# Gate and up as a two by two block product of seven products, in a decoder layer on one core

## The chip, the core and the metric

The kernel runs on one core of a Trainium2 chip. The time is the device time of one execution in microseconds. Three runs of the kernel before took 3130.09, 3134.56 and 3130.25 us; their median is 3130.25.

## What is computed

One layer of a decoder for 2048 tokens of width 1024, in float32:

```
h   = rmsnorm(x) @ w_in            -> q, k, v of two groups of heads
mix = [differential attention | stick-breaking attention]
x   = x + mix @ w_out
h2  = rmsnorm(x)
x   = x + (silu(h2 @ w_gate) * (h2 @ w_up)) @ w_down      # D_FF = 2816
out = rmsnorm(x)
```

The change touches the part from `mix @ w_out` on. Its matmuls take each float32 operand as a sum of two rounded ones, hi and lo (type float32r): a product is three matmuls, hi*hi, hi*lo and lo*hi, added up in PSUM.

## The kernel before

After projection and attention, the last part (`ffn_programs`, from L1402) goes over four blocks of 512 tokens. For each block:

- **project**: `mix` is transposed on TensorE, split into hi and lo, and multiplied with w_out in two halves of 512 output columns. The result is added to x.
- the sum is normalized, scaled into `natural`, transposed again (L1821 in block 0, L1830 in the others) and split by ScalarE (L1531) and VectorE (L1691) into `turned_hi` and `turned_lo`, 8 chunks of 128 rows x 512 tokens.
- **gate/up** (`gate_pair`, L1867): 22 tiles of 128 features. A tile is two products, gate and up, each of 8 chunks x 3 passes = 24 matmuls of 512 columns, into one PSUM bank. ScalarE takes Silu of the gate (L1543), VectorE multiplies with up (L1705), ScalarE rounds the result to `act_hi` (L1550) and VectorE makes `act_lo` (L1710). These two stay in SBUF for all 22 tiles.
- **down** (`passes`, L1788): twice 22 tiles of features, for each half of the output columns; per tile 4 token tiles x 3 passes = 12 matmuls of 512 columns. The first half of down is followed by the projection of the next block, then comes the second half, so that norms and transposes of the next block lie beside the second half.

The weights are one stream of items of 512 KB (`w_stream`), loaded by SP into two raw buffers in turn (L1444). ScalarE rounds an item to `w_hi` (128x1024, L1490, L1540, L1546) as soon as TensorE has done the item two before; VectorE subtracts to get `w_lo` (L1494, L1604); TensorE waits for `lo_split`. All engines run their instructions in the order in which they are written here, and semaphores count the steps: `multiplied` (TensorE's items), `hi_split`, `lo_split`, `silued`, `producted`. POOL has only the powers of the norms and the stores of the output in this part. `natural` of the next block is loaded early in gate/up (L1451) and x at the start of down.

Before this part begins, the last steps of attention are still under way: POOL multiplies the last weights (L1270), TensorE transposes them (L932), ScalarE copies them (L1024), TensorE multiplies with v (L946). `scalar_ahead` and `vector_ahead` split the first two items in that time (called at L1033 and L1192).

In the second part the block 0 opening is not covered by anything: TensorE has nothing else to do between its projection and its first gate matmul.

Of the kernel before, what the change touches and what calls it, by code (L numbers as in the profile page):

```python
# [22 lines left out]
P = 128  # L23
# [652 lines left out]
def attention_programs(nc, ctx, qk_scratch, v_scratch, lambdas_dram, g_mix_dram, g_mix, ident, ident_bf, causal, strict_drams,  # L676
# [3 lines left out]
    with memory:  # L680
# [516 lines left out]
        def gpsimd(pool, ahead):  # L1197
# [79 lines left out]
            def after(now):  # L1277
# [8 lines left out]
                for head in range(HEADS - 1):  # L1286
# [8 lines left out]
                    normed=S["normed"],  # L1295
                    g_ready=S["g_ready"])
# [6 lines left out]
HALF = D_MODEL // 2  # L1303
OUT_ITEMS = KC
GATE_ITEMS = 2 * FT
DOWN_ITEMS = FT // 2
PEELED = 3
PERIOD = OUT_ITEMS + GATE_ITEMS + 2 * DOWN_ITEMS
TOTAL = BLOCKS * PERIOD


def gate_item(b):
    return OUT_ITEMS + PERIOD * b


def out_item(b):
    return gate_item(b - 1) + GATE_ITEMS + DOWN_ITEMS if b else 0


def down_item(b, half):  # L1320

    between = OUT_ITEMS if b < BLOCKS - 1 else 0
    return gate_item(b) + GATE_ITEMS + half * (DOWN_ITEMS + between)


def stream_index(n):

    if n < OUT_ITEMS:
        return n
    b, at = divmod(n - OUT_ITEMS, PERIOD)  # L1330
    if at < GATE_ITEMS + DOWN_ITEMS:
        return OUT_ITEMS + at
    if b < BLOCKS - 1 and at < GATE_ITEMS + DOWN_ITEMS + OUT_ITEMS:
        return at - GATE_ITEMS - DOWN_ITEMS
    return at + (0 if b < BLOCKS - 1 else OUT_ITEMS)
# [6 lines left out]
def upper(b):  # L1342
    return 4 - lower(b)
# [10 lines left out]
def h2_bank(b, k):  # L1354
    return upper(b - 1) + k % 4 if b else k
# [6 lines left out]
def ahead_buffers(nc, ctx, H, low):  # L1362
# [5 lines left out]
    row = 4 * D_MODEL  # L1368
    small = low + (TPB + 3) * row
    F = dict(x_in=at("xin", [P, TPB, D_MODEL], keys), junk=[None, at("junk1", [P, HALF], queries)],  # L1370
             w_raw=[at(f"wraw{s}", [P, D_MODEL], values + s * row) for s in range(2)],
             natural=at("natural", [P, TPB, D_MODEL], low), g_final=at("gfinal", [P, D_MODEL], low + TPB * row),
             w_hi=[at("whi0", [P, D_MODEL], low + (TPB + 1) * row, F32R)],
             w_lo=[at("wlo0", [P, D_MODEL], low + (TPB + 2) * row, F32R)],
             g_ffn=at("gffn", [P, KC], small),
             w_loaded=[ctx.enter_context(nc.semaphore(f"f_w_loaded{s}")) for s in range(2)])
# [7 lines left out]
    assert small <= low + FENCE_BYTES  # L1384
# [17 lines left out]
def ffn_programs(nc, ctx, F, A, x, mix_scratch, w_stream, g_mix, limit, ident, out):  # L1402

    assert TOTAL % 2 == 0 and FT % 2 == 0
    memory = ExitStack()
    with memory:
        sb = lambda n, s, d=F32: memory.enter_context(nc.sbuf_tensor(n, s, d))
        sem = lambda n: ctx.enter_context(nc.semaphore(n))
        w_raw, natural, w_loaded = F["w_raw"], F["natural"], F["w_loaded"]
# [20 lines left out]

        done = lambda n: n + 2
        last = BLOCKS - 1


        turn_of = lambda which, b: b + which
        ready = KC - 1
# [588 lines left out]
```

## Time and profile before

| | |
|---|---|
| profiled execution | 3134.4 us, span 3132.6 us |
| TensorE busy | 3070.1 us, 98% |
| VectorE, ScalarE, POOL busy | 46%, 41%, 21% |
| gate/up stage of one block (four of them) | 239.36 us |
| down and projection between two gate/up stages | 170.30 us |
| mean granted TensorE clock | 0.996 of full speed |

The profile counts an engine as busy while an instruction of its own runs; TensorE's weight loads are counted apart, since they overlap its matmuls. The first 1472 us of the span are projection and attention, which stay as they are.

### The profile page before, as it was taken

The page shows a single profiled execution, that of the slowest core. Times are in us where ns is not written, and L with a number is a line of the kernel's source. Part 1 is how long each engine was busy: PE and PEld are TensorE (multiplying, and loading weights), DVE is VectorE, ACT ScalarE, POOL GpSimd, SP SyncE. Part 2 cuts the span into 40 slices and gives each one's busy share as a digit, 9 for nine tenths or more (in the row PEclk, how much of TensorE's full clock was granted, in tenths as well). Part 3 has the DMA queues.
Part 4 walks back from the last instruction along what each step waited for, and adds up shares of the span by engine and source line. Part 5 has one row for each costly group of instructions (what it writes and reads, how often), then busy time and mean ns, then how long its engine had stood idle before and what let it go on. Part 6 is the DMA issues. An engine that isn't in the chain of part 4 may idle for free.

```text
span 3132.6 us, 40561 instructions
## 1 busy us (share of the span) xinstructions
PE 3070.1 (98%) x16160; PEld 2584.0 (82%) x16160; DVE 1441.5 (46%) x1617; ACT 1294.6 (41%) x1968; POOL 669.4 (21%) x686
## 2 busy tenths in 40 slices
PE   7999999999999999999999999999999999999998
PEld 6887778787778999999888888888888888888887
DVE  6224420277676778777433333433334333343323
ACT  5122221367778887787322323322233222332222
POOL 1900000145446877775000000000000000000000
PEclk9999999999999999999999999999999999999999
DMA  5443353504444142220332322423224232233222
GB/s 197 126 122 102 94 138 92 134 18 95 108 108 93 30 108 57 53 85 15 121 99 95 121 94 94 148 96 125 94 94 148 94 119 101 96 107 108 94 101 94
DMA packets 136949, 314.77 MB, mean 100 GB/s; under 512 B 11745, under 2 KB 49377, under 8 KB 136673
## 3 DMA queue, kind: packets, MB, share of 16 engines
q1 hardware_dynamic: 134784, 305.84, 32.8%
q0 software_dynamic: 1728, 6.29, 0.5%
q8 instruction: 101, 1.65, 0.2%
q10 hardware_dynamic: 288, 0.59, 0.1%
q14 instruction: 48, 0.39, 0.0%
HBM read 253.96 MB, written 58.72 MB: 100 GB/s over the span
## 4 chain that ended last, share of the span: by engine, by line
PE 65%; DVE 7%; POOL 5%; ACT 3%; issue 1%; DVEq 0%; ACTq 0%; POOLq 0%
PE f_ps L1867 31%; PE f_ps L1788 21%; PE h_o L946 6%; PE h_t L932 3%; PE h_z L669 2%; PE h_z L672 2%; POOL h_more L1230 2%; DVE h_negmax L1066 2%; POOL h_work L1230 2%; DVE h_more L1182 2%; DVE h_more L1098 1%; ACT h_work L965 1%; ACT h_more L965 1%; POOL h_srstd L1275 1%; PE f_ps L1813 0%
## 5 line engine op out<-in xcount | busy, mean ns | idle before, releaser
L1604 DVE TENSOR_TENSOR f_wlo<-f_wraw,f_whi 128x1024 fp32r<-128x1024 f32 x294 | 360.4, 1226 | 731.6 <-ACT f_whi L1490 421.8
L1867 PE MATMUL f_ps<-f_thi,f_whi 128*128 128x512 f32 x1408 | 547.9, 389 | 0.9 <-DVE f_tlo L1691 0.9
L1867 PE MATMUL f_ps<-f_tlo,f_whi 128*128 128x512 f32 x1408 | 547.7, 389 | 0.0
L1867 PE MATMUL f_ps<-f_thi,f_wlo 128*128 128x512 f32 x1408 | 547.7, 389 | 0.0
L1270 POOL TENSOR_TENSOR h_work<-h_work,h_more 128x1024 f32<-128x1024 f32 (+3 forms) x192 | 302.5, 1587 | 110.2 <-DVE h_more L1182 97.4
L1490 ACT ACTIVATE f_whi<-f_wraw 128x1024 fp32r<-128x1024 f32 x120 | 127.1, 1060 | 459.0 <-PE f_ps L1788 456.6
L1867 PEld LDWEIGHTS f_ps<-f_thi,f_whi 128*128 128x128 f32 x1408 | 264.3, 188 | 56.3 <-issue 1.1
L1867 PEld LDWEIGHTS f_ps<-f_tlo,f_whi 128*128 128x128 f32 x1408 | 264.4, 188 | 54.9
L1867 PEld LDWEIGHTS f_ps<-f_thi,f_wlo 128*128 128x128 f32 x1408 | 264.4, 188 | 54.6
L1788 PE MATMUL f_ps<-f_whi,f_ahi 128*128 128x512 f32 x696 | 271.9, 391 | 0.0
L1788 PE MATMUL f_ps<-f_wlo,f_ahi 128*128 128x512 f32 x696 | 270.9, 389 | 0.0
L1788 PE MATMUL f_ps<-f_whi,f_alo 128*128 128x512 f32 x696 | 270.8, 389 | 0.0
L1466 POOL TENSOR_TENSOR f_rstd<-f_var,f_exponent 128x4 f32<-128x4 f32 x6 | 6.1, 1016 | 1210.4 <-DVE f_var L1663 1210.4
L946 PE MATMUL h_o<-h_v,h_attn_t 128*128 128x64 f32 x2176 | 259.7, 273 | 0.0
L946 PEld LDWEIGHTS h_o<-h_v,h_attn_t 128*128 128x128 f32 x2176 | 255.6, 193 | 0.0
L669 PE MATMUL h_z<-h_k,h_qmain 128*128 128x512 f32 (+3 forms) x576 | 223.3, 396 | 18.7 <-DVE h_more L1182 5.1
L1182 DVE TENSOR_TENSOR_SCAN h_more<-h_z,h_zero 128x1024 f32<-128x1024 f32 (+7 forms) x128 | 232.0, 1813 | 7.4
L1066 DVE TENSOR_REDUCE h_negmax<-h_z 128x1 f32<-128x1024 f32 (+7 forms) x192 | 166.5, 906 | 138.8 <-PE h_z L672 137.2
L1550 ACT ACTIVATE f_ahi<-f_gated 128x512 f32 (+1 forms) x88 | 55.6, 632 | 406.7 <-DVE f_gated L1705 406.7
L521 PE MATMUL p_ps<-p_hhi,p_whi 128*128 128x512 f32 x512 | 214.2, 418 | 0.0
L672 PE MATMUL h_z<-h_k,h_qmain 128*128 128x512 f32 (+3 forms) x576 | 213.0, 382 | 0.0
L521 PE MATMUL p_ps<-p_hhi,p_wlo 128*128 128x512 f32 x512 | 203.8, 398 | 0.0
(186 smaller groups left out, 5236.4 us busy)
## 6 DMA issues: line engine op xcount, KB each, us to landing
f_wraw<-in_w_stream SPq DMA_DIRECT2D x296, 512.0 KB, 3.2
qk_scratch<-p_ohi SPq DMA_DIRECT2D x64, 256.0 KB, 2.6
qk_scratch<-p_olo SPq DMA_DIRECT2D x64, 256.0 KB, 3.3
h_k<-qk_scratch SPq DMA_DIRECT2D x32, 512.0 KB, 8.2
h_qmain<-qk_scratch SPq DMA_DIRECT2D x64, 256.0 KB, 12.9
h_qmain<-qk_scratch SPq DMA_DIRECT2D x32, 448.0 KB, 11.0
p_wraw<-in_w_qk SPq DMA_DIRECT2D x16, 512.0 KB, 4.8
v_scratch<-p_vout SPq DMA_DIRECT2D x32, 256.0 KB, 2.0
```

The lines of the kernel that those rows point to most:

```text
L521: mm = pe.matmul(bank[o % BLOCKS][:], w[s][:, c, :], h[:, c, :], start=(c == 0 and m == 0), stop=(c == KC - 1 and m == 2))
L669: pe.matmul(out, query(m, 0, seg["tile"]), keys, start=True, stop=False)
L672: mm = pe.matmul(out, query(m, 1, seg["tile"]), keys, start=False, stop=True)
L946: mm = pe.matmul(o_bank[use % 2][:, at * HEAD_DIM:(at + 1) * HEAD_DIM], attn_t[e % 2][:, n * P:(n + 1) * P], v_sb[s][:, seg["key_tile"] + ...
L1066: done = dve.tensor_reduce(neg_max[R["set"]][:, col:col + 1], z[t["z"]][:, cols_of(seg)], AX.X, ALU.max, negate=True)
L1182: done = dve.tensor_tensor_scan(buffer[:, a:b][:, ::-1], z[cur["z"]][:, cols_of(seg)][:, ::-1], zero[:].to_broadcast([P, seg["tiles"] * P] ...
L1230: done = pool.tensor_scalar(part, part, by, neg_lam[:, 0:1], ALU.mult, ALU.mult)
L1270: done = pool.tensor_tensor(part, part, buffer[:, a + 1:b + 1], ALU.mult)
L1490: act.activation(w_hi[n % 2][:], w_raw[n % 2][:], ACT.Copy).then_inc(S["hi_split"], 1)
L1604: dve.tensor_tensor(w_lo[s][:], w_raw[s][:], w_hi[s][:].bitcast(F32), ALU.subtract)\
L1788: mm = pe.matmul(bank[outs + t][:], a[:, tok], w[s][:, cols], start=(start and n == 0), stop=(stop and n == 2))
L1867: mm = pe.matmul(bank[lower(b) + 2 * e + n][:], a[n][:, w], h[:, c, :], start=(c == 0 and m == 0), stop=(c == KC - 1 and m == 2))
```

## The change

Gate and up of a tile are computed together as one block product. The left side is w_gate and w_up, cut in two halves of the 1024 input features; the right side is h2 transposed, cut the same way, and its 512 tokens are cut in two halves of 256 (a11, a12, a21, a22). With four sums of each side there are seven products in place of eight (Winograd's form of Strassen's method). Each product is 4 chunks x 3 passes = 12 matmuls of 256 columns, and takes half a PSUM bank; a tile has 84 matmuls.

- **Weights** (`weight_sums`, POOL): t1 = up - gate of the first half, in place; t2, t3, t4 follow one from the other. Seven splits of 128x512 per tile (`gate_hi` on ScalarE, `gate_lo` on VectorE) go into a ring of seven buffers; a buffer is free when TensorE has done the product seven before. All plain weights (w_out, w_down) go through the same ring in units of 128x512.
- **Right side**: the transposed h2 is copied back from PSUM to `natural`, scaled, in float32 (`act_plain`, `dve_plain`); s1 to s4 are sums of its quarters (POOL, and VectorE in block 0). a11, a12, a22 and s1 to s4 are split in the order `PREPARED`, and TensorE takes them in the order `OPERANDS`.
- **Results** (`gate_tile`, VectorE): seven additions of 256 columns out of PSUM form gate and up; ScalarE copies the first product and takes Silu; POOL multiplies gate and up (`product`) into `act_full`, float32.
- **Down** splits the activations itself (`stage`), 128x512 at a time, into three buffers, in both halves.
- **Loads and stores**: four raw buffers in gate/up, two of which lie on the staging buffers and on t3. `natural` and x of the next block are loaded in the first half of down; the output of the block before is stored by SP in the middle of gate/up.
- `scalar_ahead` splits four units of 512; the third waits until POOL has done its last product of attention.

The core of the diff:

```diff
+OPERANDS = ["a11", "s2", "s1", "s3", "a12", "a22", "s4"]
+PREPARED = ["a11", "a12", "s2", "s1", "a22", "s3", "s4"]
...
+            def weight_sums(b, pair, e, opening=False, parts=(1, 2, 3, 4)):
+                tile, before = tile_of(b, pair, e), unit_at(b, pair, e) - PRODUCTS
+                g, u = w_raw[2 * e], w_raw[2 * e + 1]
...
+                    pool.tensor_tensor(u[:, 0:HALF], u[:, 0:HALF], g[:, 0:HALF], ALU.subtract).then_inc(S["t_made"], 1)
...
+                        pool.wait_ge(S["lo_split"], before + 2)
+                    pool.tensor_tensor(t2[:], u[:, HALF:D_MODEL], u[:, 0:HALF], ALU.subtract).then_inc(S["t_made"], 1)
...
+                        pool.wait_ge(S["lo_split"], before + 4)
...
+                    pool.tensor_tensor(t3[:], t2[:], g[:, 0:HALF], ALU.subtract).then_inc(S["t_made"], 1)
...
+                        pool.wait_ge(S["lo_split"], before + 6)
+                    else:
+                        pool.wait_ge(S["side_lo"], PRODUCTS * (b + 1))
+                    pool.tensor_tensor(t4[:], g[:, HALF:D_MODEL], t2[:], ALU.subtract).then_inc(S["t_made"], 1)
...
+            def product(b, pair, e):
+                pool.wait_ge(S["silued"], tile + 1)
+                pool.wait_ge(S["added"], tile * 7 + 7)
+                pool.tensor_tensor(here, gated[:], up[:], ALU.mult).then_inc(S["act_made"], 1)
...
+                with pool.Fori(1, pairs - 1) as pair:
+                    weight_sums(b, pair, 1)
+                    product(b, pair - 1, 1)
+                    weight_sums(b, pair + 1, 0)
+                    product(b, pair, 0)
...
         def scalar_ahead(act):
-            for n in range(2):
-                split_hi(act, n)
+            for u in range(4):
+                if u == 2:
+                    act.wait_ge(A["multiplied"], A["steps"])
+                plain_hi(act, u)
...
+            def gate_lo(b, pair, e, i):
+                split_lo(dve, (gate_unit(b) + i) % RING, unit_at(b, pair, e) + i, gate_source(e, i))
+            def gate_tile(b, pair, e, extra=None, opening=False, closing=False):   # VectorE
+                for i in range(PRODUCTS):
+                    if i:
+                        dve.wait_ge(S["multiplied"], u + i + 1)
+                    if i == 1:
+                        add(second[:], held[1][:, low], first[:])
+                    if i == 2:
+                        add(third[:], held[2][:, low], second[:])
+                    if i == 3:
+                        add(fourth[:], held[3][:, low], second[:])
+                        add(up[:, high], held[2][:, low], fourth[:])
+                    if i == 4:
+                        add(gate[:, low], held[0][:, high], first[:])
+                    if i == 5:
+                        add(gate[:, high], held[1][:, high], fourth[:])
+                    if i == 6:
+                        add(up[:, low], held[2][:, high], third[:])
+                    if closing:
+                        if i in (2, 3, 4):
+                            stage(b, i - 2)
+                        plain_lo(dve, gate_unit(b) + GATE_UNITS + i)
...
+                        gate_lo(b, pair + e, 1 - e, i)
...
-                        for c in range(KC):
-                            for m, (a, h) in enumerate(((w_hi, turned_hi), (w_lo, turned_hi), (w_hi, turned_lo))):
-                                mm = pe.matmul(bank[lower(b) + 2 * e + n][:], a[n][:, w], h[:, c, :],
+                    for c in range(4):
+                        col = slice(c * P, (c + 1) * P)
+                        for m, (w, a) in enumerate(((w_hi, side_hi), (w_lo, side_hi), (w_hi, side_lo))):
+                            mm = pe.matmul(outs[i], w[ring][:, col], a[name][:, c, :], start=(c == 0 and m == 0),
```

## Rows read from the trace of the kernel before

**Rows 1.** The page: busy time of each engine, and the chain by engine.
```profile
PE 3070.1 (98%) x16160; PEld 2584.0 (82%) x16160; DVE 1441.5 (46%) x1617; ACT 1294.6 (41%) x1968; POOL 669.4 (21%) x686
...
PE 65%; DVE 7%; POOL 5%; ACT 3%; issue 1%; DVEq 0%; ACTq 0%; POOLq 0%
PE f_ps L1867 31%; PE f_ps L1788 21%; PE h_o L946 6%; PE h_t L932 3%; PE h_z L669 2%; PE h_z L672 2%; POOL h_more L1230 2%; DVE h_negmax L1066 2%; POOL h_work L1230 2%; DVE h_more L1182 2%; DVE h_more L1098 1%; ACT h_work L965 1%; ACT h_more L965 1%; POOL h_srstd L1275 1%; PE f_ps L1813 0%
```
**Rows 2.** Busy time of each engine in gate/up of block 1.
```profile
core 0: us, PE busy (x) PEld busy (x) DVE busy (x) ACT busy (x) POOL busy (x), PEclk, DMA share, GB/s
1945.62:2184.98 239.36, 239.36 (x1058) 198.26 (x1057) 90.45 (x96) 70.75 (x95) 3.41 (x5) 1.00 0.36 123
```
**Rows 3.** The chain of waits in time order, block 1 (start us, us, what).
```profile
1945.62 239.36 PE f_ps L1867 x1056
...
2210.26 114.27 PE f_ps L1788 x504
```
**Rows 4.** Timeline of TensorE (start us, us): score matmuls, the first and fourth of a row.
```profile
664.05 0.28 PE L672 MATMUL h_z<-h_k,h_qmain 128*128 128x256 f32 x1
...
664.41 0.40 PE L669 MATMUL h_z<-h_k,h_qmain 128*128 128x512 f32 x1
```
**Rows 5.** Busy time in two stretches of 64-wide matmuls, columns as in rows 2.
```profile
1472.58:1475.90 3.32, 3.32 (x19) 3.32 (x18) 0.00 (x0) 1.02 (x1) 0.00 (x0) 0.50 0.00 0
1477.60:1481.36 3.76, 3.76 (x34) 3.76 (x34) 0.00 (x0) 1.02 (x1) 0.00 (x0) 0.95 0.00 0
```
**Rows 6.** Groups by form, ScalarE (xcount, busy us, mean ns, idle before).
```profile
L1550 ACT ACTIVATE f_ahi<-f_gated 128x512 f32 x64 | 40.5, 632 | 302.9 <-DVE f_gated L1705 302.9
L1490 ACT ACTIVATE f_whi<-f_wraw 128x1024 fp32r<-128x1024 f32 x120 | 127.1, 1060 | 459.0 <-PE f_ps L1788 456.6 <-DMA f_wraw<-in_w_stream 2.4
L982 ACT ACTIVATE h_out<-h_o 128x256 f32<-128x256 f32 x16 | 5.2, 383 | 2.1 <-PE h_o L889 2.1
```
**Rows 7.** Groups by form, VectorE.
```profile
L1604 DVE TENSOR_TENSOR f_wlo<-f_wraw,f_whi 128x1024 fp32r<-128x1024 f32 x294 | 360.4, 1226 | 731.6 <-ACT f_whi L1490 421.8 <-ACT f_whi L1546 295.4 <-ACT f_whi L1540 6.2
L1710 DVE TENSOR_TENSOR f_alo<-f_gated,f_ahi 128x512 f32 x64 | 44.4, 693 | 59.3 <-ACT f_ahi L1550 59.3
L1617 DVE TENSOR_TENSOR f_xin<-f_ps,f_xin 128x512 f32<-128x512 f32 x32 | 20.0, 683 | 6.2 <-PE f_ps L1788 6.1
L1172 DVE TENSOR_TENSOR h_z<-h_z,h_drop 128x128 f32<-128x128 f32 x128 | 38.0, 297 | 91.8 <-ACT h_z L1016 91.6
```
**Rows 8.** Groups by form, POOL.
```profile
L1251 POOL TENSOR_TENSOR h_out<-h_out,h_rstd 128x512 f32<-128x512 f32 x16 | 16.6, 1040 | 1.3
L281 POOL TENSOR_TENSOR p_cos<-p_cos,p_part 128x1024 f32<-128x1024 f32 x2 | 4.8, 2400 | 0.2
```
**Rows 9.** Timeline of VectorE and POOL at two places where they overlap.
```profile
132.83 3.40 DVE L420 TENSOR_TENSOR p_wlo<-p_wraw,p_whi 128x1024 fp32r<-128x1024 f32 x1 [0.19 <-ACT p_whi L307]
...
132.76 2.39 POOL L286 TENSOR_TENSOR p_sin<-p_sin,p_part 128x1024 f32<-128x1024 f32 x1
...
1468.89 3.67 DVE L1494 TENSOR_TENSOR f_wlo<-f_wraw,f_whi 128x1024 fp32r<-128x1024 f32 x2 [0.62 <-ACT f_whi L1490]
```
**Rows 10.** Timeline between the projection of block 0 and its first gate matmul.
```profile
1530.69 3.88 PE L1821 MATMUL f_ps<-ident_sb,f_natural 128*128 128x128 f32 x32 [0.87 <-DVE f_xin L1617]
...
1535.46 0.47 PE L1867 MATMUL f_ps<-f_thi,f_whi 128*128 128x512 f32 x1 [0.89 <-DVE f_tlo L1691]
```
**Rows 11.** Timeline at the end of attention.
```profile
1468.36 2.00 POOL L1270 TENSOR_TENSOR h_work<-h_work,h_more 128x1024 f32<-128x1024 f32 x1 [0.62 <-DVE h_more L1182]
...
1469.71 1.00 ACT L1024 ACTIVATE h_attn_t<-h_t 128x1024 f32<-128x1024 f32 x1
1470.86 1.72 PE L932 MATMUL h_t<-ident_sb,h_work 128*128 128x128 f32 x8 [1.43 <-ACT h_attn_t L1024]
```
**Rows 12.** DMA issues: xcount, KB each, median us from issue to landing.
```profile
f_wraw<-in_w_stream SPq DMA_DIRECT2D x296, 512.0 KB, 3.2
...
f_natural<-mix_scratch SPq DMA_DIRECT2D x3, 2048.0 KB, 9.2
```

More of the change, by code:

```diff
@@ L1354, in h2_bank, with first_h2 @@
 def h2_bank(b, k):
-    return upper(b - 1) + k % 4 if b else k
+    return upper(b - 1) + k % 4
+def first_h2(k, half):
+    return 4 * half + k // 2, slice(k % 2 * BLK // 2, (k % 2 + 1) * BLK // 2)
 MIX_AHEAD = D_MODEL - COLS
@@ L1484, in gpsimd @@
[L1484 to L1494 removed]
+            high_sums(0)
@@ new lines, in gate_tile @@
+            def gate_tile(b, pair, e, extra=None, opening=False, closing=False):
+                tile, u = tile_of(b, pair, e), unit_at(b, pair, e)
+                first_bank = bank[(upper if e else lower)(b)]
+                for i in range(PRODUCTS):
+                    act.wait_ge(S["multiplied"], u + i + 1)
+                    if i == 0:
+                        if opening:
+                            act.wait_ge(S["side_lo"], PRODUCTS * (b + 1))
+                        if not opening or b:
+                            act.wait_ge(S["added"], tile * 7 - 2)
+                        act.activation(first[:], first_bank[:, 0:SIDE], ACT.Copy).then_inc(S["first_copied"], 1)
+                    if i == 6:
+                        if not opening or b:
+                            act.wait_ge(S["act_made"], tile)
+                        act.wait_ge(S["added"], tile * 7 + 6)
+                        act.activation(gated[:], gate[:], ACT.Silu).then_inc(S["silued"], 1)
+                    if extra is not None:
+                        extra(i)
+                    if closing:
+                        if i in (2, 3, 4):
+                            stage(b, i - 2)
+                        plain_hi(act, gate_unit(b) + GATE_UNITS + i)
+                    elif opening:
+                        for k in NEXT_TILE_STEPS.get(i, ()):
+                            gate_hi(b, pair, 1, k)
+                    else:
+                        gate_hi(b, pair + e, 1 - e, i)
@@ L1591, in scalar @@
             square(0, 0, 1, range(TPB))
-            h2_hi(0, range(KC))
+            first_plain()
+            prepare_hi(0, "a11")
+            prepare_hi(0, "a12")
+            act_plain(0, range(4))
+            for name in PREPARED[2:]:
+                prepare_hi(0, name)
             for b in range(BLOCKS):
@@ L1730, in down @@
[L1730 to L1743 removed]
+                    dve.wait_ge(S["h2_turned"], b * KC + (k if b else k | 1) + 1)
@@ L1871, in gate_up @@
[L1871 to L1876 removed]
+                    mm = passes(u, turned_hi[:, c, :], turned_lo[:, c, :], out_bank(b, half), c == 0, c == KC - 1)
+                    mm.then_inc(S["multiplied"], 1)
+                    if b == 0 and k == 4:
+                        mix_turns(0, range(ready, KC))
```

752 lines of the change are left out of this document (488 added, 264 removed).

## The prediction

> **What bounds the kernel now.** I read the shares of busy time first: TensorE is at 98%, every other engine under half, and the chain that ended last runs through TensorE for 65% of the span, 31% on the gate/up matmuls of L1867 alone [rows 1]. Then the stages. In a gate/up stage of one block TensorE is busy for all of 239.36 us and VectorE for only 90.45, ScalarE 70.75 [rows 2]; the chain has 1056 matmuls there in one piece with no wait, and the down stage beside it is the same (504 in 114.27) [rows 3]. So the second half of the kernel is TensorE's own rate and nothing else: 239.36/1056 = 0.2267 us for 512 columns with their weight load. The four gate/up stages take 4 x 239.4 = 958 us. What the change gains, it gains there; what it adds counts only where TensorE comes to wait.
>
> **The products.** Before, a tile of 128 features takes 2 x 8 x 3 = 48 matmuls of 512 columns, 10.88 us. After, it takes 7 x 4 x 3 = 84 matmuls of 256 columns, so 7392 over the 88 tiles. The columns fall by one eighth, but each matmul still loads 128x128 weights. The trace has the form in the score matmuls: 256-wide matmuls of a row start at 664.05, .17 and .29 and the next one at .41, 0.12 apart [rows 4]. The bound from below is the weight load itself: 64-wide matmuls come every 3.76/34 = 0.111 us [rows 5]. From above, 0.125 allows for the waits that now stand after each 12 matmuls instead of 24. 512 columns at 2.4 GHz are 213 ns and take 227, so 256 (107 ns) plus the same 13 is 120; I take 0.119, or 84 x 0.119 = 10.0 us a tile and 880 us in all (820 to 924): 78 less than before. Half the columns cost more than half the time, so of the 120 us that an eighth of 958 would be, only these 78 are there.
>
> The Trainium skill ("TensorE: Matmul & The Clock Gate", Back-to-back issue gap) gives sustained spacings of about 131 ns at 512 columns and 81 at 128; that is an estimate of 98 ns at 256 and would make the stages 724 us. The trace has 227 and 111, so its figures are not these matmuls' and I leave them out.
>
> **What the other engines must do in those 10.0 us.** ScalarE: seven roundings of 128x512 at 0.63 [rows 6], one copy of 256 columns out of PSUM at 0.38, one Silu 0.63: 5.4 us. It is no bound. VectorE: seven remainders of 128x512 at 0.69, and seven additions of 256 columns from PSUM; 512 take 0.683 and 128 take 0.297, so 256 about 0.43 [rows 7]: 4.85 + 2.98 = 7.8 us. POOL, idle in these stages until now, gets four subtractions and a product of 128x512. Its rows: 1.04 for a product of 512, but an addition of 1024 takes 2.40, so about 1.28 for 512 [rows 8]: 4 x 1.28 + 1.04 = 6.2 us. Each alone fits in 10.0.
>
> They are not alone. Where a VectorE op with two SBUF inputs meets a POOL tensor op, one stands until the other ends: at 132.83 a VectorE subtraction took 3.40 us, where 1.23 is usual, since POOL's addition ran from 132.76 to 135.15. At 1468.89 two VectorE splits took 3.67, where two alone take 2.45, with POOL's product running until 1470.36 [rows 7, 9, 11]. The blocked op does its first 0.14 us meanwhile: 1.08 after POOL's end, against 1.23 alone. The additions out of PSUM are not of this kind; L1617, PSUM and SBUF, stays at 0.68 beside POOL.
>
> The Trainium skill ("SBUF — State Buffer", SBUF: two separate sides) has this as a rule: the port pair that the two share is an exclusive lock, also for a VectorE op with two SBUF inputs against a GpSimd op that reads SBUF. By that rule, the trace agrees, and it speaks against this change.
>
> So VectorE's seven splits hold the port for 7 x 0.55 = 3.9 us a tile and POOL's five for 4 x 1.14 + 0.90 = 5.5: 9.4 of 10.0. A POOL op that waited for a split starts as the split ends, beside the next addition (0.43 + 0.14 = 0.57 us of cover); what is longer falls on VectorE: 4 x 0.57 + 0.33 = 2.6. VectorE would be at 7.8 + 2.6 = 10.4 us a tile at the worst of this pattern, and at 7.8 at best. Step 3 has two additions in a row and hides one op whole, and ops without a dependence overlap a little. The ring of seven gives six products of slack, so no single delay shows, only the sum. I take 10.2 us a tile (10.0 to 10.4; 88 tiles: 898 us): 60 less than before.
>
> **The opening of block 0.** Before, 32 transposes begin at 1530.69 and the first gate matmul at 1535.46 [rows 10]. After: the transposes of two tiles end at 1532.5; ScalarE's eight copies of 256 (0.38) at 1535.6; rounding of a11 (1.06), remainder (1.23) [rows 6, 7]: the first product starts at 1538.0. The second wants s2, behind the remainder of a12, four more copies (1541.0), two sums of 1.23, rounding and remainder: 1545.8. Then one remainder of 1.23 after the other: s1, a22, s3 and s4 end at 1550.8. t4 overwrites cells that these read, so it comes after them: POOL 1.28, rounding, remainder, 1553.5; two products more: 1556.4. With everything ready it would be 1535.5 + 10.0. That is **+11 us** (8 to 15). TensorE is idle for some 10 us of this; the trace has a stretch at a granted clock of 0.50 (1.2 of 2.4 GHz), just after TensorE had waited 1.43 us for a copy [rows 11], and 19 matmuls took 3.32 us in it, 0.175 each instead of 0.111 [rows 5]. Such a stretch may come here: **+2** (0 to 6).
>
> **The end of attention.** Splits ahead are four of 512 instead of two of 1024, and the third waits for POOL's last product. That product ends at 1470.36, and ScalarE's next copy, which TensorE waits 1.43 us for, now starts at 1469.71 [rows 11]. After: 1470.4 + 2 x 0.63, so 1471.7: **+2** (0 to 2.5).
>
> **Down and projection.** Their matmuls are unchanged, 0.2267 each. Down now splits its activations itself, 22 tiles twice: per unit of 12 matmuls (2.72 us) ScalarE 1.26, VectorE 1.38. That hides. The two loads of 2 MB move from gate/up into the first half of down, where weight loads queue behind them; they land in 9.2 us, a weight load in 3.2 [rows 12], and the ring has six units (16 us) of slack: 0 (to 4 a block). In the second half, the four last transposes now wait for copies that begin after unit 7: ScalarE 0.83 + 0.63 + 1.38, VectorE behind it 3.8 us, against a unit of 2.72: 1.1 a block. In units 10 to 16 VectorE has 0.69 + 0.69 + 1.23 = 2.6 of 2.72, and POOL's four sums of 1024 (2.4 each) hold the port beside it; 9.6 us of holding against 5.4 of slack in the three staging buffers: 2.5 a block (0 to 8). Three blocks: **+11**. The next block's first tile, whose two loads wait for the last two down units: 1 each, **+3**. From gate/up into down, the third bank waits for the last addition, which is late behind the closing splits: 0.7 x 4 = **+3**.
>
> Output stores go from POOL's queue to SP's; they have the whole stage: 0.
>
> **Sum.** 898 - 958 = -60; +11 +2 +2 +11 +3 +3 = +32; -28. The profiled execution took 3134.4 (span 3132.6), so 3106; the median of the runs, 3130.25, is 4 lower, so **3102 us**. From no change, a measurement here tells about 0.2%, 6 us.
>
> **Rivals.**
> - *The port is absorbed* (0.22). VectorE finds its gaps, gate/up runs at 10.0 a tile: -78, and with little waiting in down (+20): 3134 - 58 = 3076, by the median 3072. For it: VectorE's own work is 7.8. Against: 9.4 of 10.0 port time leaves nearly nothing.
> - *The port becomes the bound* (0.26), slower. Place: each gate/up tile. If POOL's ops meet splits and not additions, each costs VectorE up to its whole 1.0 to 1.1: 13 us a tile at the very worst; with half of that, and POOL's own chain waiting for VectorE's splits, 11.0: 968, +10, +32: 3176, by the median 3172. It decides from (958 - 32)/88 = 10.5 us a tile, a tenth above my own upper bound. For it: rows 9. Against: additions and POOL ops align by themselves.
> - *The preparation in down eats it* (0.07). If VectorE falls behind from unit 10 on by the whole 9.6 us in each of three blocks: +21 more, 3123 to 3130, no change.
>
> **How the numbers follow.** Forecast 0.45 (3082 to 3122). Faster: 0.45 + 0.22; same 0.07; slower 0.26. With under 0.1 left out on each side, 3062 (absorbed, 0.118 a matmul, less than +20) to 3168 (tile at about 11).
>
> **What would show it.** 256-wide matmuls at 0.118 to 0.120 where none waits; TensorE's busy share in a gate/up stage under 100% and the stage at 224 us instead of 239; VectorE splits of 128x512 with a mean well over 0.69 (0.9 to 1.1) and VectorE near full; first product 2.5 us later and tile 0 some 20 us long; waits before transposes in down. I am wrong if 256 columns take 0.13 or more, if splits stay at 0.69 beside POOL, or if TensorE waits for weights' DMA.

## The result, and the profile after

The changed kernel takes 3215.87 us (median of 4 runs, 3213.1 to 3220.71) against 3130.58 for the kernel before (3130.09 to 3134.56): 1.0271 times, 95% interval 1.0253 to 1.0289. I had forecast 3102, with a range of 3062 to 3168; the kernel is slower, and the time lies above the range.

The page of the changed kernel, busy time and chain, against [rows 1]:

```profile
PE 3048.6 (95%) x19328; PEld 2695.7 (84%) x19328; DVE 2227.4 (69%) x2807; ACT 1602.5 (50%) x2724; POOL 1410.1 (44%) x1128
...
PE 23%; DVE 14%; issue 6%; POOL 6%; DMA 1%; DVEq 0%; ACT 0%; POOLq 0%; SPq 0%; ACTq 0%
PE f_ps L2108 18%; DVE f_wlo L1665 9%; PE f_ps L2207 5%; POOL f_act L1606 2%; POOL f_t L1599 2%; DVE f_gate L1972 1%; DMA f_wraw<-in_w_stream 1%; DVE f_up L1972 1%; DVE f_third L1972 1%; DVE f_fourth L1972 1%; POOL f_t L1586 1%; POOL f_wraw
```

TensorE is still busy 95% of the span, but its gate/up matmuls have fallen out of the chain: L2207 holds 5% of it where L1867 held 31%. VectorE's splits (L1665) and POOL's operations stand there instead. Block 1's gate/up stage (us from start to end of the stretch, then each engine's busy time, granted clock, DMA) says which engine has no slack:

```profile
1984.88:2235.05 250.17, 228.68 (x1850) 223.05 (x1849) 244.27 (x320) 115.03 (x208) 166.06 (x106) 0.99 0.30 102
```

In [rows 2] TensorE was busy for the whole stage and VectorE for 90.45 of 239.36. Now VectorE is busy for 244.27 of 250.17 and TensorE waits. The groups of this stretch (count, busy us, mean ns, idle before) show what fills it, against [rows 7] and [rows 8]:

```profile
L1665 DVE TENSOR_TENSOR f_wlo<-f_wraw,f_whi 128x512 fp32r<-128x512 f32 x90 | 114.2, 1286 | 1.5 <-ACT f_whi L1747 1.4
L1665 DVE TENSOR_TENSOR f_wlo<-f_t,f_whi 128x512 fp32r<-128x512 f32 x64 | 75.0, 1172 | 1.5 <-ACT f_whi L1747 1.5
...
L1599 POOL TENSOR_TENSOR f_t<-f_wraw,f_t 128x512 f32<-128x512 f32 x21 | 34.6, 1648 | 4.4 <-DVE f_wlo L1665 4.4
...
L1606 POOL TENSOR_TENSOR f_act<-f_gated,f_up 128x512 f32 x18 | 31.9, 1774 | 0.0
L1581 POOL TENSOR_TENSOR f_wraw<-f_wraw,f_wraw 128x512 f32<-128x512 f32 x21 | 30.0, 1428 | 56.7 <-DMA f_wraw<-in_w_stream 56.7
...
L1972 DVE TENSOR_TENSOR f_second<-f_ps,f_first 128x256 f32<-128x256 f32 x22 | 9.0, 411 | 0.0
```

A split of 128x512 takes 0.68 us when nothing is beside it; here the mean is 1.24 (the 90 of 1286 ns and the 64 of 1172 taken together). The additions out of PSUM keep their 0.41. One tile in the timelines of VectorE and then POOL (start us, us), as in [rows 9]:

```profile
2156.42 1.79 DVE L1665 TENSOR_TENSOR f_wlo<-f_t,f_whi 128x512 fp32r<-128x512 f32 x1
2158.14 0.41 DVE L1972 TENSOR_TENSOR f_gate<-f_ps,f_first 128x256 f32<-128x256 f32 x1
2158.47 1.45 DVE L1665 TENSOR_TENSOR f_wlo<-f_wraw,f_whi 128x512 fp32r<-128x512 f32 x1
2159.84 0.41 DVE L1972 TENSOR_TENSOR f_gate<-f_ps,f_fourth 128x256 f32<-128x256 f32 x1
2160.17 1.45 DVE L1665 TENSOR_TENSOR f_wlo<-f_t,f_whi 128x512 fp32r<-128x512 f32 x1
...
2156.38 1.29 POOL L1581 TENSOR_TENSOR f_wraw<-f_wraw,f_wraw 128x512 f32<-128x512 f32 x1 [2.15 <-DMA f_wraw<-in_w_stream]
2157.83 1.53 POOL L1586 TENSOR_TENSOR f_t<-f_wraw 128x512 f32<-128x512 f32 x1 [0.17 <-POOL f_wraw L1581]
2159.53 1.55 POOL L1593 TENSOR_TENSOR f_t<-f_t,f_wraw 128x512 f32<-128x512 f32 x1 [0.16 <-POOL f_t L1586]
```

The two alternate strictly: POOL ends at 2157.67, the split that started beside it 0.54 later, at 2158.21; POOL at 2159.36, the next split 0.56 later. The addition between two splits covers only 0.33 us of POOL's operation.

The granted clock is not what sets this pace: in 2100 to 2200 it was 1.00 throughout, VectorE was busy for 99.69 of the 100 us, and a tile took 10.6 to 11.4 us.

The 82.0 us by which the span grew (3132.6 to 3214.6), stage by stage from the first and last matmul of each (a neighbour's last matmul and the next first one overlap by 0.16 us):

| stretch | before | after | difference | forecast |
|---|---|---|---|---|
| to the first projection matmul | 1485.55 | 1488.12 | +2.6 | +2 |
| from there to the first gate matmul | 49.91 | 63.48 | +13.6 | +2.5 of the opening's +13 |
| four gate/up stages | 958.4 | 1003.3 | **+44.9** | **-60**, and the other +10.5 of the opening |
| three times down and projection between them | 510.4 | 530.2 | +19.8 | +17 |
| last down stage | 128.3 | 129.5 | +1.2 | 0 |

### The profile page after: what moved, and what is told of

Read it like the earlier page. It is cut to its first block, busy times and chain, and to the rows that moved or that the text cites. A ratio compares the mean times of both kernels' runs of the same rounds, so it can differ in the third digit from the quotient of the medians.

```text
span 3214.6 us, 52829 instructions
## 1 busy us (share of the span) xinstructions
PE 3048.6 (95%) x19328; PEld 2695.7 (84%) x19328; DVE 2227.4 (69%) x2807; ACT 1602.5 (50%) x2724; POOL 1410.1 (44%) x1128
## 4 chain that ended last, share of the span: by engine, by line
PE 23%; DVE 14%; issue 6%; POOL 6%; DMA 1%; DVEq 0%; ACT 0%; POOLq 0%; SPq 0%; ACTq 0%
PE f_ps L2108 18%; DVE f_wlo L1665 9%; PE f_ps L2207 5%; POOL f_act L1606 2%; POOL f_t L1599 2%; DVE f_gate L1972 1%; DMA f_wraw<-in_w_stream 1%; DVE f_up L1972 1%; DVE f_third L1972 1%; DVE f_fourth L1972 1%; POOL f_t L1586 1%; POOL f_wraw L1581 1%; DVE f_slo L1962 0%; POOL f_sum_s L1622 0%; DVE f_second L1972 0%
## 5 line engine op out<-in xcount | busy, mean ns | idle before, releaser
L1665 DVE TENSOR_TENSOR f_wlo<-f_wraw,f_whi 128x512 fp32r<-128x512 f32 x592 | 631.0, 1077 | 114.9 <-ACT f_whi L1656 104.2
L2207 PE MATMUL f_ps<-f_hi_s,f_whi 128*128 128x256 f32 x1408 | 408.4, 290 | 63.5 <-DVE f_up L1972 58.9
L2207 PE MATMUL f_ps<-f_lo_s,f_whi 128*128 128x256 f32 x1408 | 400.6, 285 | 0.0
L2207 PE MATMUL f_ps<-f_hi_s,f_wlo 128*128 128x256 f32 x1408 | 400.1, 284 | 0.0
L2207 PEld LDWEIGHTS f_ps<-f_hi_s,f_whi 128*128 128x128 f32 x1408 | 271.5, 193 | 79.2 <-DVE f_up L1972 68.4
L2207 PE MATMUL f_ps<-f_hi_a,f_whi 128*128 128x256 f32 x1056 | 304.5, 288 | 22.3 <-DVE f_second L1972 13.2
L1665 DVE TENSOR_TENSOR f_wlo<-f_t,f_whi 128x512 fp32r<-128x512 f32 x264 | 304.2, 1152 | 11.5 <-ACT f_whi L1747 11.5
L2207 PE MATMUL f_ps<-f_hi_a,f_wlo 128*128 128x256 f32 x1056 | 301.9, 286 | 0.0
L2207 PE MATMUL f_ps<-f_lo_a,f_whi 128*128 128x256 f32 x1056 | 301.8, 286 | 0.0
L2108 PE MATMUL f_ps<-f_whi,f_shi 128*128 128x512 f32 x696 | 275.3, 396 | 7.7 <-DVE f_slo L1962 7.7
L2108 PE MATMUL f_ps<-f_whi,f_slo 128*128 128x512 f32 x696 | 273.6, 393 | 0.0
L2207 PEld LDWEIGHTS f_ps<-f_hi_s,f_wlo 128*128 128x128 f32 x1408 | 271.8, 193 | 0.0
L2207 PEld LDWEIGHTS f_ps<-f_lo_s,f_whi 128*128 128x128 f32 x1408 | 271.7, 193 | 0.0
## 6 DMA issues: line engine op xcount, KB each, us to landing
h_qmain<-qk_scratch SPq DMA_DIRECT2D x32, 448.0 KB, 10.8
```

Source lines behind the costliest of these rows:

```text
L1665: dve.tensor_tensor(w_lo[ring][:], source, w_hi[ring][:].bitcast(F32), ALU.subtract).then_inc(S["lo_split"], 1)
L2108: mm = pe.matmul(bank[outs + t][:], a[:, tok], w[u % RING][:], start=(start and n == 0), stop=(stop and n == 2))
L2207: mm = pe.matmul(outs[i], w[ring][:, col], a[name][:, c, :], start=(c == 0 and m == 0), stop=(c == 3 and m == 2))
```

## The experiments

Every experiment is a single execution unless a number of runs is given. The four runs of the changed kernel lie 7.6 us apart, so where two versions differ by less than that, the stages' lengths in the traces carry the reading and not the execution's time.

The theory: a VectorE operation with two SBUF inputs and a POOL operation exclude each other (the port), and with five POOL operations a tile VectorE has become the bound at 11.4 us. Rivals: the order of the seven products (each waits for an addition or copy of an earlier one); the raw weights, for which POOL waits 56.7 us in the stage above; and POOL's own work, 166.06 us of 250.17, which with that wait nearly fills the stage.

**Sums of 32 columns.** In `weight_sums`, for all tiles but a block's first:
```
-  pool.tensor_tensor(t2[:], u[:, HALF:D_MODEL], u[:, 0:HALF], ALU.subtract)
+  pool.tensor_tensor(t2[:, 0:32], u[:, HALF:HALF + 32], u[:, 0:32], ALU.subtract)
```
and the same for the three others.

> The changed kernel with GpSimd's four weight sums of every tile but the block's first only 32 columns wide instead of 512 (the same number of instructions and the same waits; the combinations are left out of the other 480 columns, so the result is not the reference's). The product gate times up stays as it is. Theory 1 (VectorE is held off by GpSimd's float32 sums at the shared port until it is the gate/up bound): the splits fall from a mean of 1.08 us to near 0.70-0.80, VectorE's busy share in the gate/up windows falls from 98% to below 85%, a tile from 11.4 us to 10.0-10.5, and the four gate/up stages from 1003 to 880-925 us; the execution ends near 3090-3140. Theory 2 (the order of the seven products, each of which waits for an addition or a copy of the one before, sets 11.4 us whatever the splits cost): the tile stays over 11.0. Theory 3 (GpSimd waits for the raw weights, and the tile with it): stays over 11.0 too.

Measured: 3105.61 us; the stages 230.9 (block 0) and 220.16 three times, 10.007 us a tile. Block 1's stage:

```profile
1960.93:2181.08 220.15, 220.15 (x1850) 220.15 (x1849) 186.06 (x320) 118.33 (x208) 59.66 (x106) 1.00 0.34 116
```

TensorE is busy for all of it, with the waits of `added` and `first_copied` in place: the order of the products costs nothing once VectorE is quick, and that rival falls. 220.15/1848 is 0.1191 us a matmul. The splits' mean is 0.81 us, just above the 0.80 expected: the product gate times up is still 512 wide, and 21 of the 153 splits take over 1.3 us. This run shortens POOL's own work too (59.66 us busy), so by itself it doesn't tell the exclusion from a POOL that is too slow; the version with three operands over PSUM does.

**A quarter of the loads.**
```
-  sp.dma_start(w_raw[slot + part][:], w_stream[stream + part])
+  sp.dma_start(w_raw[slot + part][:, cols], w_stream[stream + part][:, cols])   # cols: 256 of 1024, from tile 2 on
```

> The changed kernel with the loads of the gate and up weights, from the third tile of a block on, cut to the first 256 of 1024 columns (the other columns keep older weights, so the result is not the reference's). Every engine's instructions are unchanged. Theory 1 (port): GpSimd's waits for loads (26 us in a 100 us stretch) go away, and since it is VectorE that has no slack the tile stays at 11.2-11.5 us, the execution within 10 us of 3215. Theory 3 (the loads, freed late by the last reader of the ring's slot, hold the chain): the tile falls by 0.5 us or more, four stages by over 40 us, the execution to below 3175. Theory 2 (order of the products): no change.

Measured: 3209.67 us; block 1's stage 248.01, where it was 250.17; VectorE is still busy for 238.97 of it. The four stages are 2.1, 2.1, 0.5 and 0.9 us shorter, 5.7 in all, although POOL's waits for loads in 2100 to 2200 fell from 26.0 to 14.8 us. POOL's waits for them are idle time of an engine that is not the bound.

**Three operands over PSUM.** ScalarE copies the source of steps 1, 3 and 5 of each steady tile into the idle bank 3 of the other parity, and the split reads that:
```
+  act.wait_ge(S["lo_split"], ...)                                    # the copy before has been read
+  act.activation(spare(b, e), gate_source(e, i), ACT.Copy).then_inc(S["spared"], 1)
...
+  pe.wait_ge(S["lo_split"], u + (VIA[-1] if i == 3 and not opening else i) + 1)   # TensorE writes that bank from step 3 on
...
-  dve.tensor_tensor(w_lo[ring][:], gate_source(e, i), w_hi[ring][:].bitcast(F32), ALU.subtract)
+  dve.tensor_tensor(w_lo[ring][:], spare(b, e), w_hi[ring][:].bitcast(F32), ALU.subtract)
```

> The changed kernel with nothing left out: in the steady gate/up tiles ScalarE first copies the source of three of the seven operands (a float32 copy of 128x512 into an idle PSUM bank), and VectorE's split of these three reads that bank in place of SBUF, so that it has only one input in SBUF. ScalarE's work grows by 3 copies of 0.63 us a tile, from 5.4 to 7.3 us. Theory 1 (port): VectorE's splits that read PSUM run at 0.65-0.75 us instead of 1.08 and GpSimd's sums are held off less; VectorE's busy time falls by about 1.1 us a tile, the tile from 11.4 to 10.2-10.7 us, the execution to 3115-3150. Theory 2 (order of the products): the added copy and wait lengthen each of the three steps, the tile 11.4-12.0, the execution 3215-3270. Theory 3 (loads): no gain either, 3205-3230.

Measured: 3133.96 us, 82 less than the changed kernel. Block 1's stage, and in a second view the groups of splits in it:

```profile
1961.18:2191.26 230.08, 224.00 (x1850) 222.28 (x1849) 215.58 (x321) 146.36 (x268) 163.53 (x106) 0.99 0.32 111
```
```profile
L1675 DVE TENSOR_TENSOR f_wlo<-f_wraw,f_whi 128x512 fp32r<-128x512 f32 x91 | 116.3, 1294 | 5.0 <-ACT f_whi L1761 4.8
L1675 DVE TENSOR_TENSOR f_wlo<-f_ps,f_whi 128x512 fp32r<-128x512 f32 x60 | 40.7, 679 | 4.8 <-ACT f_whi L1761 4.7
```

The splits with one input in PSUM take 679 ns beside the same POOL operations that make 1294 of the others. Nothing is left out here and ScalarE is busy 1.4 us a tile more, yet the stage is 20 us shorter: what hurt was the two inputs in SBUF. POOL's work is the same as before (163.53 us busy), so it was not POOL's own length that held the tile. What is left of the loss lies in the first seven tiles of the stage. From the eighth on TensorE is busy all the time, at 10.0 to 10.3 us a tile:

```profile
2040.20:2191.26 151.06, 151.06 (x1263) 150.49 (x1262) 143.86 (x215) 100.05 (x181) 106.14 (x71) 1.00 0.33 115
```

**All seven over PSUM.** The same with seven steps.

> As the run before, with all seven operands of a steady tile copied to the idle PSUM bank first: ScalarE's work is 5.4+7x0.63=9.8 us a tile, and each copy waits for the split before it, as there is one bank for them. Theory 1 (port): no split has two SBUF inputs any more, so splits run at 0.65-0.75 us and GpSimd's sums at their undisturbed 1.3 us; VectorE's busy share falls to near 75%; but the chain copy, rounding copy, split of 0.63+0.63+0.70 us and their hand-overs, seven times, is about 14 us a tile if it is never overlapped and 10 if it is: I expect 10.5-12 us, the execution 3130-3270. Theories 2 and 3: splits keep a mean above 0.95 us, the execution above 3215.

Measured: 3450.11 us, above the whole range; the stages take 305 to 312 us. VectorE, in the same columns as before:

```profile
2149.41 0.69 DVE L1675 TENSOR_TENSOR f_wlo<-f_ps,f_whi 128x512 fp32r<-128x512 f32 x1 [1.34 <-ACT f_whi L1761]
2150.02 0.41 DVE L1988 TENSOR_TENSOR f_second<-f_ps,f_first 128x256 f32<-128x256 f32 x1
2151.41 0.69 DVE L1675 TENSOR_TENSOR f_wlo<-f_ps,f_whi 128x512 fp32r<-128x512 f32 x1 [0.98 <-ACT f_whi L1761]
```

The splits are as fast as expected, but one starts only every 2.0 us: copy, rounding, split in a row through one bank, 7 x 2.0 = 14 us a tile. That is the number that the expectation gives for the case without overlap. The mechanism was as expected there, the overlap was not: ScalarE's copies and VectorE's splits wait for each other (38.0 and 43.9 us in 100).

**POOL operations beside the kernel before.** In block 0's gate/up stage, from tile 2 on; the three versions differ in one line (ten operations a tile in the third):
```
+  pool.tensor_tensor(junk[0][:], junk[0][:], junk[0][:], ALU.add)                             # one buffer twice
+  pool.tensor_tensor(junk[0][:], junk[0][:], x_sum[0][:, 0, 0:HALF], ALU.add)                 # two buffers
+  pool.tensor_tensor(junk[0][:, 0:256], junk[0][:, 0:256], junk[0][:, 256:HALF], ALU.add)     # two halves of one
```

> The kernel before the change, with five float32 additions of 128x512 on GpSimd (zeros, into a buffer that nothing uses then) beside each of the tiles 2 to 21 of block 0's gate/up stage, and nothing beside the three other blocks' stages. Theory 1 (port): VectorE's 128x1024 splits in block 0 rise from 1.23 us to 1.6-2.4 us in the mean, while those of the other blocks stay at 1.23; but VectorE was busy 90 of 239 us there, so that even with all of GpSimd's 20x5x1.3 = 130 us added it has room: the stage stays within 2 us of the others', the execution within 4 us of 3131. That is the same contention as in the changed kernel, made free by VectorE's slack. If the two engines don't exclude each other, the splits stay at 1.23 us and theory 1 has to go. The reading that contention costs time wherever it is: block 0's stage over 5 us longer than the others'.

> The kernel before the change again with five GpSimd additions of 128x512 beside each tile of block 0's gate/up stage, now of two different inputs (the buffer and a piece of the layer's input) instead of one buffer twice. The run before with one buffer twice left VectorE's splits at 1.225 us although they ran beside GpSimd. If it is GpSimd's reading of two different streams that holds VectorE off, the splits of block 0 rise to a mean of 1.6-2.4 us and the stage stays within 2 us of the others', since VectorE has the slack, the execution within 4 us of 3131. If the splits stay at 1.23 us here too, the exclusion is not a matter of GpSimd's addition as such, and what held VectorE off in the changed kernel has to be sought in its operands' places or in the order in which the two engines start.

> The kernel before with ten GpSimd additions of 128x256 beside each of block 0's gate/up tiles 2 to 21: first half of a buffer of zeros plus its second half, so the same buffer and the same data as in the run that added one buffer to itself (VectorE's splits 1.225 us), but two different streams of addresses as in the run with two buffers (1.70 us). If it is the two different input streams that exclude VectorE, the 128x1024 splits of block 0 come to a mean of 1.4-1.8 us. If it was the data (zeros) or the buffer's place, they stay at 1.23 us. The execution stays at 3128-3135 us in either case.

Measured: 3134.44, 3131.07 and 3134.22 us, and block 0's stage 239.86, 239.90 and 239.88 (239.87 without any of it). The splits in 1560 to 1770, in the order of the three:

```profile
L1613 DVE TENSOR_TENSOR f_wlo<-f_wraw,f_whi 128x1024 fp32r<-128x1024 f32 x39 | 47.8, 1226 | 67.1 <-ACT f_whi L1553 64.2 <-ACT f_whi L1547 0.9
```
```profile
L1613 DVE TENSOR_TENSOR f_wlo<-f_wraw,f_whi 128x1024 fp32r<-128x1024 f32 x39 | 68.1, 1745 | 53.4 <-ACT f_whi L1553 50.5 <-ACT f_whi L1547 1.0
```
```profile
L1613 DVE TENSOR_TENSOR f_wlo<-f_wraw,f_whi 128x1024 fp32r<-128x1024 f32 x39 | 64.2, 1646 | 60.0 <-ACT f_whi L1553 57.7
```

The first expectation failed: the splits stayed at 1.23 us, and by its own words that speaks against the theory. The two other runs, which hit theirs, show that the theory holds for two different inputs and was too wide. In the first run 19 of the 39 splits overlap one of POOL's operations and take 1225 ns like the others; in the other two nearly all of them overlap one. Two results. Contention is free where VectorE has slack: splits 0.4 to 0.5 us longer, the stage unchanged. And a POOL addition that reads one buffer twice holds nobody off; with two different inputs, of the same buffer or of two, it does.

**The next block's activation sums on VectorE**, with the three copies kept (`s1` to `s4` in down, at units 10, 11, 12 and 14).
```
+  if k in (10, 11, 12, 14):
+      later_sum(b + 1, {10: "s1", 11: "s2", 12: "s3", 14: "s4"}[k])    # dve.tensor_tensor, was pool.tensor_tensor
```

> As the kernel with three copies to the idle PSUM bank (3133.96 us), and in the down stage the four activation sums of the next block (s1 to s4) run on VectorE instead of GpSimd. Theory 1 in that place: there a split of 0.69 us beside a GpSimd sum took 2.9 us, one sum took 9.2 us, and the stretch of 156 matmuls before the next gate/up stage took 39.5 us where 156x0.227 = 35.4 are due. With the sums on VectorE (4 of about 1.2 us) no operation is held off there, the stretch falls to 35.5-37.5 us, three times: 6-12 us in all, the execution 3121-3129, below the kernel before. Rival: the preparation's own length (seven roundings and seven remainders in order) holds the stretch: it stays at 39-41 us, and the execution at 3132-3140.

Measured: 3126.5 us; the stretch of 156 matmuls takes 35.9 to 36.0. VectorE and POOL in the changed kernel there:

```profile
1951.37 2.91 DVE L1962 TENSOR_TENSOR f_slo<-f_act,f_shi 128x512 fp32r<-128x512 f32 x1 [0.19 <-ACT f_shi L1737]
1954.21 2.88 DVE L1665 TENSOR_TENSOR f_wlo<-f_wraw,f_whi 128x512 fp32r<-128x512 f32 x1
1957.02 3.42 DVE L1952 TENSOR_TENSOR f_lo_a<-f_natural,f_hi_a 128x1024 fp32r<-128x1024 f32 x1
...
1951.33 2.41 POOL L1611 TENSOR_TENSOR f_sum_s<-f_natural 128x1024 f32<-128x1024 f32 x1 [21.05 <-DVE f_natural L1937]
1953.82 2.73 POOL L1613 TENSOR_TENSOR f_sum_s<-f_sum_s,f_natural 128x1024 f32<-128x1024 f32 x1
1956.50 2.85 POOL L1619 TENSOR_TENSOR f_sum_s<-f_natural 128x1024 f32<-128x1024 f32 x1
1965.19 8.60 POOL L1622 TENSOR_TENSOR f_sum_s<-f_natural,f_sum_s 128x1024 f32<-128x1024 f32 x1 [5.84 <-DVE f_lo_s L1957]
```

and VectorE in this version:

```profile
1932.76 0.69 DVE L1991 TENSOR_TENSOR f_slo<-f_act,f_shi 128x512 fp32r<-128x512 f32 x1 [0.19 <-ACT f_shi L1745]
1933.37 0.68 DVE L1673 TENSOR_TENSOR f_wlo<-f_wraw,f_whi 128x512 fp32r<-128x512 f32 x1
1933.97 1.22 DVE L1956 TENSOR_TENSOR f_sum_s<-f_natural 128x1024 f32<-128x1024 f32 x1
```

Three VectorE operations that take 2.6 us alone took 9.1. Giving VectorE a sum of 1.22 us spares it a wait of up to 2.2 for POOL's.

**Four operands over PSUM** (steps 0, 2, 4, 6), otherwise the same.

> As the run before, but four of seven operands (0, 2, 4, 6) take the way over PSUM instead of three (1, 3, 5). Theory 1: VectorE, still busy 96% with three, gets another 0.4 us a tile free and a tile falls from 10.43 to 10.1-10.3 us, the execution another 5-25 us lower. Rival: the one bank that all copies share serialises ScalarE's copy and VectorE's split (with seven of seven the execution was 3450 us): a tile of 10.6-11.5 us, the execution 10-90 us higher.

Measured: 3123.58 us, 2.9 less, under what the theory gave and by itself within the noise: 227.4 to 227.8 us a stage (10.35 a tile), where three had 228.4 to 230.0. VectorE's busy time fell from 214.4 to 184.0 us in block 1's stage; from the eighth tile on a tile took 10.0 to 10.4 us with three copies already, so freeing VectorE more brings little.

**Block 0's s3 and s4 on VectorE too.**
```
-  high_sums(0)                # pool
+  later_sum(0, "s3")          # dve, after low_sums()
+  if name == "s2": later_sum(0, "s4")      # in the loop over the preparation
```

> The version with four of seven operands over PSUM and the next block's activation sums on VectorE (3123.58 us in one run), with block 0's sums s3 and s4 on VectorE as well. Theory 1: at the opening of block 0 the remainders and GpSimd's sums stand in each other's way too (PE waited 4.0 us for a remainder there and the stage took 236.3 us against 227.5 of the others); with the sums on VectorE that wait goes and block 0's stage falls by 2-8 us, the execution to 3115-3122 us, a ratio to the kernel before of 0.995-0.998. Rival: the opening is bound by the length of the preparation and by the clock after it (0.50 in 14 us there), not by who does the sums: no change, 3121-3126 us, a ratio of 0.997-0.999.

Measured: 3118.28 us (3115.33 to 3119.51, 4 runs), 0.9951 of the kernel before (0.9934 to 0.9967). Block 0's stage fell from 236.3 to 231.8.

**The second tile of a block over PSUM as well.**
```
-  gate_hi(b, pair, 1, k)
+  gate_hi(b, pair, 1, k, True)      # and gate_lo; ScalarE first waits for act_plain, dve_plain and x2_half
```

> The version with all activation sums on VectorE and four of seven operands over PSUM (3118.28 us), in which the second tile of every block, too, has its four operands copied to the idle PSUM bank (before, only the tiles from the third on had it). In that version's trace the matmuls of a block's later tiles stand 0.119 us apart without gaps, but between the first tiles of each block PE has gaps of 2.2, 1.1 and 0.4 us and then 3.4 us at half its clock, while VectorE's splits beside GpSimd's sums take 1.3-1.8 us: about 8 us a block. Theory 1: without the exclusion there these gaps shrink to under 1 us and the clock stays at 1.0: 4-8 us a block, the execution 3088-3106 us, ratio 0.987-0.992. Rival: in the first tiles it is VectorE's own load that counts (the four additions of 0.68 us of the block before stand in front of the first tile's), the added copies change nothing: 3112-3122 us, ratio 0.995-0.997.

Measured: 3111.31 us (3109.52 to 3112.28, 5 runs), 0.9935 of the kernel before (0.9922 to 0.9949). A stage of blocks 1 to 3 is 225.8 to 226.0 us, where it was 227.5 to 228.3: 2 us a block, not 4 to 8, and the execution is just below the rival's 3112 and above the theory's 3106, so most of that loss at the start of a stage is something else. TensorE's waits in block 1's stage (in total, times, longest):

```profile
PE f_ps L2247 <- DVE f_up L2007: 2.7, 4, 1.5
PE f_ps L2247 <- DVE f_wlo L1672: 0.4, 1, 0.4
```

Of the 5.6 us over 220.2, 3.1 are in these waits, and the rest in gaps between matmuls that are too short to be listed as waits. It isn't the clock, which was granted at 1.00 for the whole of this stage. It isn't the later tiles either, as the stage cut at the start of its ninth tile shows:

```profile
1955.76:2041.36 85.60, 82.40 (x674) 80.52 (x673) 70.04 (x121) 57.47 (x110) 60.73 (x41) 1.00 0.30 106
2041.36:2181.52 140.16, 140.16 (x1179) 140.16 (x1178) 107.24 (x200) 100.19 (x182) 92.81 (x66) 1.00 0.35 117
```

All of it lies in the second to the eighth tile, which take 10.2 to 11.8 us; the later ones take 10.0. At this place VectorE also finishes the block before: the four additions that the rival names, and four operations of 1.99 us that scale the output (L1934). Block 0 has no block before it, and its tiles from the third on take 10.0. So this work fits as the cause, but no run moves it. This is the fastest version, 0.65% under the kernel before: the changes are in who does what, none in the arithmetic of the products.

**Only the sums moved**, no copies.

> The changed kernel with only the activation sums moved from GpSimd to VectorE and no operand copied to PSUM. The stages add: the down stretch of 156 matmuls before a gate/up stage falls from 39.5-40.3 us to 36 (3x4 = 12 us in all), block 0's stage by 2-5 us, and the steady tiles stay at 11.2-11.4 us: 3198-3206 us. If the parts do not add, because a VectorE ahead of its work at the start of the stage would keep ahead: below 3190.

Measured: 3201.79 us: down 35.9 to 36.0, the steady stages still 247.5 to 250.3. The parts add: the sums are worth 14 us here and three copies 82 by themselves, 96 together, and the version with all sums moved and four copies is 97.6 under the changed kernel, the same within the noise.

## Why the prediction was wrong

- **The step that failed** is "A POOL op that waited for a split starts as the split ends, beside the next addition (0.43 + 0.14 = 0.57 us of cover)", and with it the 2.6 us a tile of waiting and the 10.2 us tile. The count was nearly right: 96 of the stage's 153 splits, 4.4 a tile, take over 1.3 us, so met a POOL operation, of which there are five. Each such split takes 1.57 us, 0.89 more than alone; I had 0.57 for a subtraction and 0.33 for the product. That is 3.9 us a tile. The cover is 0.33 at best, since an operation starts 0.08 before the one ahead of it ends, and where POOL starts with the split itself there is none (1.79 instead of 0.68). The product of 128x512 on POOL was too short as well: 1.29 us where nothing holds it, not 1.04. VectorE comes to 244.27/22 = 11.1 us a tile, above my "worst of this pattern" of 10.4, and the 87 tiles behind the opening take 11.3 us in the mean. I had set two streams' lengths side by side and trusted them to align; they do alternate, but the one that waits is VectorE. The stages carry 94 of the 111 us between the forecast for the profiled execution (3106) and its time (3216.7).
- A term that I didn't have: in the first seven tiles of blocks 1 to 3 VectorE also finishes the block before, 2.5 us in four additions (L1862) and 8.2 in four operations that scale the output (L1918). The second to the seventh tile there take 12.5 us in the mean, the later ones 10.9. With narrow sums both take 10.0, so whatever makes this difference costs only where VectorE has no slack; that it is this work is likely and not shown.
- The rival "the port becomes the bound" had place, mechanism and point of decision (10.5 us a tile) right, and its tile of 11.0 was close; its 3172 was still too low, and lay just above the end of my range, 3168. I gave it 0.26, when port holding of 9.4 out of 10.0 us spoke for it.
- The products: right. 0.1191 us a matmul where none waits, 220.15 us a stage; so 10.0 a tile and -77 were there to be had, and the 10.8 more of block 0, in the version with narrow sums, are its opening.
- The opening of block 0 (+13 with the clock) was too small, and that it is close to the 13.6 of the table above is chance. Three pieces make it up. The first is in no term: within the projection TensorE waits 5.1 us, and with the half clock that follows its transposes begin 8.0 us later after the first projection matmul than before. The wait is for the last transposed piece of `mix`. ScalarE rounds it (L1698) behind four roundings of weights (L1656), and those weights were loaded only when the store of `mix` had landed, at 1502.86; before, the same rounding (L1525) stood ahead of the late weights. ScalarE after, then before:

```profile
1506.42 2.41 ACT L1656 ACTIVATE f_whi<-f_wraw 128x512 fp32r<-128x512 f32 x4 [14.52 <-DMA f_wraw<-in_w_stream]
1508.73 0.67 ACT L1698 ACTIVATE f_thi<-f_ps,g_mix 128x512 fp32r<-128x512 f32 x1
```
```profile
1499.91 0.69 ACT L1525 ACTIVATE f_thi<-f_ps,g_mix 128x512 fp32r<-128x512 f32 x1 [2.04 <-PE f_ps L1813]
1502.96 1.06 ACT L1490 ACTIVATE f_whi<-f_wraw 128x1024 fp32r<-128x1024 f32 x1 [2.36 <-DMA f_wraw<-in_w_stream]
```

  The loads waited for that store before as well (they were issued at 1499.32); what differs is the order on ScalarE. All ten traces with the new opening have this wait (5.0 to 5.3 us), where the kernel before waits 1.1; no run moves the order, so this cause is read from the traces and not tested. So TensorE did come to wait for a load of weights, my third sign of being wrong, but here and not in the gate/up tiles. The second piece is +5.6 from the transposes to the first gate matmul, where I had 2.5: it waits for all copies of h2 out of PSUM, not only for a11's remainder. The third is the first tile, 21.6 us in place of 10.0, where I had 18.4 and 2 for the clock; TensorE waits 4.0 in it for the remainder of a sum, and there is a stretch at 0.50 of the clock, of the kind in [rows 5] (columns as above):

```profile
1545.20:1551.60 6.40, 0.00 (x1) 0.03 (x1) 4.10 (x7) 4.55 (x9) 0.12 (x1) 0.83 0.00 0
1551.60:1560.00 8.40, 4.44 (x19) 4.17 (x20) 7.24 (x5) 3.90 (x4) 4.89 (x2) 0.50 0.00 0
```

  Together that is 25 us against the 13, and 11.6 of it lies inside the +44.9 of the stages.
- Down (+17 with the next block's first tile and the third bank): +19.8, with the parts off. The stretch beside the preparation cost 4.9, 4.7 and 4.1 us a block, not 2.5; the wait before the transposes 0.8, not 1.1. The next block's first tile takes 10.0 us, so its +3 was nothing, and the third bank's +3 does not show at all. Some 1.2 us a block remain, in matmuls that stand slightly further apart (0.2288 us for 0.2267 in the longest piece); the last down stage has the same 1.2, and why is open. The 0 for loads held.
- End of attention (+2): +2.6 in these two traces, but single executions differ by as much there. The first projection matmul starts at 1482.1 to 1485.6 in four traces with the old opening and at 1486.4 to 1491.2 in ten with the new one, so the sign is right and the size is not settled.

## What to carry to other kernels

Before work goes to an idle POOL, add up the port: every VectorE operation with two SBUF inputs plus every POOL operation with two; where that sum comes near the stage's length, count what each meeting costs VectorE (here 0.89 us for a POOL operation of 1.3) and hope for no alignment. Then look for what else the fuller engine does in some tiles only, and for what stands behind a late load in an engine's order. The cure is to change where an operand lies, not who is faster: a split that reads PSUM (a ScalarE copy of 0.6 us) is free of it, and a sum that VectorE did itself in 1.22 us was cheaper to it than the same sum done by POOL. And look where the contention lands: the same meetings cost the kernel before nothing, as VectorE was busy there for 38% of the stage.

## What was not expected of the hardware

- A POOL addition with the same buffer as both inputs (1.21 us for 128x512) ran beside a VectorE split of two SBUF inputs with no effect on it (1226 ns); with two different inputs the split took 1745 and 1646, and POOL's operation 1.57. The Trainium skill ("SBUF — State Buffer", SBUF: two separate sides) lets any GpSimd operation that reads SBUF exclude such a VectorE operation; the first of the three runs differs from that, and the measurement decides; I have no run on why.
- The exclusion works both ways, but not evenly: one POOL sum of 128x1024 took 8.60 us, as in the last row of POOL above, where the first one took 2.41; meanwhile eight VectorE operations with two SBUF inputs followed each other without a gap, none of them longer than alone (0.68 and 1.21 us).
- Half the columns cost 0.119 to 0.2267, that is 53%; with 84 matmuls of 256 for 48 of 512 the product saves 8%, not 12.5%.
